# One stage of a fused two-block kernel: an output turned by TensorE is instead moved between partitions by small DMAs

## The reference

```
u  = h @ w_in                                   # 256 x 1024
bu = einsum('sbgk,gpk->sbgp', u by groups, b)   # complex: 64 groups, 64 states each, 16 inputs each
x_t = a * x_{t-1} + bu_t                        # complex diagonal recurrence over the 256 positions
y  = Re(einsum('sbgp,gkp->bsgk', x, c)) + d_skip * u
y  = gelu(y)
y  = y * sigmoid(y @ w_glu)
out = y @ w_o
```

## Time and profile before

| | before |
|---|---|
| median of three runs | 2977.66 us (2976.47 to 2978.38) |
| the profiled execution's own time | 2976.47 us |
| its span | 2974.7 us |
| TensorE busy | 2838.1 us (95%) |
| VectorE busy | 1879.9 us (63%) |
| ScalarE busy | 1341.9 us (45%) |
| mean granted TensorE clock | 0.971 of full speed |

### The profile page before, as it was taken

How to read it: one execution, slowest core, us unless ns; L and a number is a source line. 1 busy time by engine, 2 the same in 40 slices (tenths; PEclk the granted TensorE clock), 3 DMA queues, 4 the chain that set the end, 5 groups by cost and what they waited for, 6 DMA issues and landing times.

```text
span 2974.7 us, 42854 instructions
## 1 busy us (share of the span) xinstructions
PE 2838.1 (95%) x17486; PEld 2547.6 (86%) x17487; DVE 1879.9 (63%) x2146; ACT 1341.9 (45%) x1380; POOL 275.3 (9%) x248
## 2 busy tenths in 40 slices
PE   6988999898999999999998999999999999998999
PEld 4857988887888888888877998888899999996999
DVE  5474454546898888887453653785566466485655
ACT  1222431215777777776443432343544444345444
POOL 0002862300000000000001000002100010010000
PEclk8968999898999999999999999999999999999999
DMA  7845674355999999998462563433456456472553
GB/s 238 272 158 151 187 222 134 96 197 192 336 376 336 341 341 377 335 340 315 170 211 87 180 202 118 141 114 113 133 183 201 139 170 208 150 186 80 181 180 110
DMA packets 504835, 609.84 MB, mean 205 GB/s; under 512 B 50201, under 2 KB 371836, under 8 KB 504700
## 3 DMA queue, kind: packets, MB, share of 16 engines
q1 hardware_dynamic: 502224, 606.82, 61.1%
q10 hardware_dynamic: 2476, 1.06, 0.1%
HBM read 605.75 MB, written 1.05 MB: 204 GB/s over the span
## 4 chain that ended last, share of the span: by engine, by line
PE 85%; DVE 5%; DMA 3%; issue 2%; ACT 2%; POOL 1%; SPq 0%; DVEq 0%; ACTq 0%; POOLq 0%
PE bank L1423 31%; PE bank L1986 7%; PE bank L1832 4%; PE bank L1836 4%; PE bank L1845 4%; PE bank L1250 4%; PE bank L1745 3%; PE bank L1302 3%; PE bank L1894 2%; PE bank L1885 2%; PE bank L1886 2%; DMA ring<-in_o_exp_down 1%; PE bank L1750 1%; PE bank L1920 1%; DVE ring L3085 1%
## 5 line engine op out<-in xcount | busy, mean ns | idle before, releaser
L3189 DVE TENSOR_TENSOR ring_r<-ring,store_area_r 128x2048 fp32r<-128x2048 f32 (+1 forms) x344 | 805.5, 2379 | 228.0 <-ACT store_area_r L2397 225.1
L2397 ACT ACTIVATE store_area_r<-ring 128x2048 fp32r<-128x2048 f32 (+1 forms) x344 | 665.5, 1971 | 235.9 <-PE bank L1423 81.3
L1423 PE MATMUL bank<-sq_r,store_area_r 128*128 128x256 f32 x1648 | 241.6, 288 | 13.0 <-ACT sq_r L2401 8.0
L1423 PE MATMUL bank<-sq_r,ring_r 128*128 128x256 f32 x1664 | 236.4, 285 | 0.0
L1423 PE MATMUL bank<-hT_r,store_area_r 128*128 128x256 f32 x1648 | 233.3, 285 | 0.0
L1423 PEld LDWEIGHTS bank<-sq_r,store_area_r 128*128 128x128 f32 x1648 | 217.1, 193 | 18.5 <-issue 9.0
L1986 PE MATMUL bank<-hT,ring 128*128 128x256 f32 x1024 | 230.0, 380 | 0.0
L3631 DVE TENSOR_TENSOR ring_r<-ring,store_area_r 128x3072 fp32r<-128x3072 f32 x64 | 195.0, 3088 | 47.2 <-ACT store_area_r L2795 47.2
L1423 PEld LDWEIGHTS bank<-sq_r,ring_r 128*128 128x128 f32 x1664 | 217.4, 194 | 0.0
L1423 PEld LDWEIGHTS bank<-hT_r,store_area_r 128*128 128x128 f32 x1648 | 214.8, 194 | 0.0
L1986 PEld LDWEIGHTS bank<-hT,ring 128*128 128x128 f32 x1024 | 190.8, 190 | 27.1 <-issue 3.1
(11 more groups left out here) (545 smaller groups left out, 4762.6 us busy)
## 6 DMA issues: line engine op xcount, KB each, us to landing
ring<-in_o_exp_gate SPq DMA_DIRECT2D x88, 1024.0 KB, 7.1
ring<-in_o_exp_up SPq DMA_DIRECT2D x88, 1024.0 KB, 7.2
ring<-in_ffn_w_gu SPq DMA_DIRECT2D x88, 1024.0 KB, 6.7
ring<-in_o_exp_down SPq DMA_DIRECT2D x32, 1536.0 KB, 8.5
ring<-in_ffn_w_down SPq DMA_DIRECT2D x32, 1408.0 KB, 8.7
ring<-in_o_exp_down SPq DMA_DIRECT2D x32, 1280.0 KB, 11.3
ring<-in_ssd_w_in SPq DMA_DIRECT2D x32, 1024.0 KB, 7.1
ring<-in_e_mod_mix_w SPq DMA_DIRECT2D x12, 1024.0 KB, 9.1
```

Source lines behind the costliest of these rows:

```text
L1423: i = mm(out, w(k), x(k), start=(p == k == 0), stop=(p == 2 and k == blocks - 1))
L2397: activation(dst, slot(u, s, kk), ACT.Copy).then_inc(w_high, 1)
L3189: nc.vector.tensor_tensor(slot(u, s, kk, rounded=True), slot(u, s, kk), as_f(high), ALU.subtract).then_inc(w_low, 1)
```

## The change

The output y gets the orientation in which the inputs came: rows (j, 32 features) and columns (b, t). The tables become the stationary side with 128 columns, and the state and `u` the moving side with 63 and 64. ACT copies PSUM (128 x 256) in one piece to one of four `y_raw` buffers, and then 16 DMAs for each tile (`outputs_moved`), of 32 partitions x 256 bytes each, bring it to rows (b, 32 features): 8 issued by SP, 8 by ACT. The transposes on PE are gone. The semaphore `moved` becomes two. The skip sum of tile j comes one round later on DVE, and waits for the DMAs. The state is stored unshifted, in contiguous tiles. On PE the two later halves of the `u` product move into the loop, one in m = 0 and one in m = 1; on ACT the evacuation of tiles 4 to 7 and its DMAs follow the copy and the DMAs of tile 0. On SP the loads for glu 1 and two mod units are placed between the DMAs.

```
+    def outputs_moved(eng, issue, m, phases):
+        eng.wait_ge(moved[m % 2], MOVES * (m // 2 + 1))
+        for j in phases:
+            for b in range(4):
+                issue.dma_start(y_nat(m)[32 * b:32 * b + 32, j * S5_B:(j + 1) * S5_B],
+                                y_raw(m)[32 * j:32 * j + 32, b * S5_B:(b + 1) * S5_B]).then_inc(moved[m % 2], 16)
...
-    y_raw = lambda m, h: ring[0:S5_B, 2 * (m % 2) + h, (KD + 2) * COLS:(KD + 3) * COLS]
+    y_raw = lambda m: ring[:, m % 4, (KD + 2) * COLS:(KD + 3) * COLS]
...
                 if stage == "s5_glu":
                     glu_units(0, 1)
-                    sp.wait_ge(evac, base["s5_in"] + 2)
-                    inputs_moved(sp, nc.sync, 1, (0, 1))
-                    glu_units(1, 4)
+                    for m in range(S5_M):
+                        if m == 1:
+                            sp.wait_ge(evac, base["s5_in"] + 2)
+                            inputs_moved(sp, nc.sync, 1, (0, 1))
+                            glu_units(1, 3)
+                        sp.wait_ge(y_cp, m + 1)
+                        outputs_moved(sp, nc.sync, m, (0, 1))
+                    glu_units(3, 4)
...
-                    pe.wait_ge(moved, MOVES * (m // 4 + 1))
+                    pe.wait_ge(moved[m // 4], MOVES)
...
-                    y = y_banks[m % 2][0:S5_B, :].rearrange("p (j b c) -> p j b c", j=S5_L, b=4)
+                    y = y_banks[m % 2]
                     for b in range(4):
-                        at = slice(b * S5_B, (b + 1) * S5_B)
-                        mm(y[:, :, b, :], u_rel(m)[:, at], s5_direct(m)[:, b, :].rearrange("p (j c) -> p j c", c=32), start=True, stop=False)
+                        i, at = 4 * m + b, b * S5_B
+                        mm(y[:, at:at + S5_B], s5_direct(m)[:, b, :], u_rel(m)[:, at:at + S5_B], start=True, stop=False)
                         for n in range(2):
-                            ins = mm(y[:, :, b, :], s5_p[m % 2][:, n, at], s5_ct[n][:, 4 * m + b, :, :], start=False, stop=(n == 1))
+                            ins = mm(y[:, at + 1:at + S5_B], s5_ct[n][:, i, :, :].rearrange("p j c -> p (j c)"),
+                                     s5_p[m % 2][:, n, at:at + S5_B - 1], start=False, stop=(n == 1))
...
-                for s in range(2):
-                    later_half(s)
-                pe.wait_ge(bc_cp, before + S5_M)
                 for m in range(S5_M):
+                    if m < 2:
+                        later_half(m)
                     if m + 2 < S5_M:
                         inputs(m + 2)
                     outputs(m)
-                    if m >= 1:
-                        outputs_turned(m - 1)
-                outputs_turned(S5_M - 1)
...
-                unit_in(1)
                 for m in range(S5_M):
+                    if m == 1:
+                        unit_in(1)
                     se.wait_ge(w_used, m + 1)
-                    if m >= 2:
-                        se.wait_ge(y_turned, m - 1)
-                    for half in range(2):
-                        ins = activation(y_raw(m, half), y_banks[m % 2][0:S5_B, half * T:(half + 1) * T], ACT.Copy)
-                    ins.then_inc(y_cp, 1)
+                    if m >= 4:
+                        se.wait_ge(y_read, m - 3)
+                    activation(y_raw(m), y_banks[m % 2][:, 0:T], ACT.Copy).then_inc(y_cp, 1)
+                    se.wait_ge(y_cp, m + 1)
+                    outputs_moved(se, nc.scalar, m, (2, 3))
                     if m >= 2:
                         gelu(m - 2)
...
-                    if m >= 4:
-                        j = m - 4
-                        ve.wait_ge(y_turned, j + 1)
-                        nc.vector.scalar_tensor_tensor(out=y_nat(j), in0=u_nat(j), scalar=vcol("o_d_skip", j), in1=y_turn(j),
+                    if m >= 5:
+                        j = m - 5
+                        ve.wait_ge(moved[j % 2], MOVES * (j // 2 + 2))
+                        nc.vector.scalar_tensor_tensor(out=y_nat(j), in0=u_nat(j), scalar=vcol("o_d_skip", j), in1=y_nat(j),
```

More of the change, by code:

```diff
@@ L149, in program @@
     (s5_act, s5_dve, s5_tr, s5_cols, range_ready, ple_half, tab_ready, raw_in, c_raw_in, b0_ready, bw_ready, c_exp, c_powers,
-     bc_tr, bc_cp, y_cp, y_turned) = (sem(n) for n in (
+     bc_tr, bc_cp, y_cp) = (sem(n) for n in (
         "s5_act", "s5_dve", "s5_tr", "s5_cols", "range_ready", "ple_half", "tab_ready", "raw_in", "c_raw_in", "b0_ready",
-        "bw_ready", "c_exp", "c_powers", "bc_tr", "bc_cp", "y_cp", "y_turned"))
-    moved = sem("moved")
+        "bw_ready", "c_exp", "c_powers", "bc_tr", "bc_cp", "y_cp"))
+    moved = [sem(f"moved{i}") for i in range(2)]
     bu_ready, bu_turned, turned, scanned, back_c, w_ready, w_used, y_read, y_gelu, glu_sig = (
@@ L320, in inputs_moved @@
                 issue.dma_start(to[:, :, b * S5_B:(b + 1) * S5_B],
-                                act[32 * b:32 * b + 32, 4 * i:4 * i + 4, j * S5_B:(j + 1) * S5_B]).then_inc(moved, 16)
+                                act[32 * b:32 * b + 32, 4 * i:4 * i + 4, j * S5_B:(j + 1) * S5_B]).then_inc(moved[i], 16)
+    def outputs_moved(eng, issue, m, phases):
[4 more added lines that the diff above has]
+                                y_raw(m)[32 * j:32 * j + 32, b * S5_B:(b + 1) * S5_B]).then_inc(moved[m % 2], 16)
     EPS_COL, FB_COL, DTB_COL, ALOG_COL = 0, 1, 2, 3
@@ L442, in program @@
     v_banks, d_banks, y_banks = (bank_x, bank_sum), banks[d_set:d_set + 2], banks[y_set:y_set + 2]
-    y_turn = lambda m: (d_banks if m < S5_M - 2 else v_banks)[m % 2][:, 0:T]
     BT_CHUNKS, C_CHUNKS = 2 * S5_M, 4
@@ L1661, in outputs @@
                     pe.wait_ge(back_c, m + 1)
-                    y = y_banks[m % 2][0:S5_B, :].rearrange("p (j b c) -> p j b c", j=S5_L, b=4)
+                    y = y_banks[m % 2]
                     for b in range(4):
-                        at = slice(b * S5_B, (b + 1) * S5_B)
-                        mm(y[:, :, b, :], u_rel(m)[:, at], s5_direct(m)[:, b, :].rearrange("p (j c) -> p j c", c=32), start=True, stop=False)
+                        i, at = 4 * m + b, b * S5_B
+                        mm(y[:, at:at + S5_B], s5_direct(m)[:, b, :], u_rel(m)[:, at:at + S5_B], start=True, stop=False)
                         for n in range(2):
-                            ins = mm(y[:, :, b, :], s5_p[m % 2][:, n, at], s5_ct[n][:, 4 * m + b, :, :], start=False, stop=(n == 1))
+                            ins = mm(y[:, at + 1:at + S5_B], s5_ct[n][:, i, :, :].rearrange("p j c -> p (j c)"),
+                                     s5_p[m % 2][:, n, at:at + S5_B - 1], start=False, stop=(n == 1))
                     ins.then_inc(w_used, 1)
-                def outputs_turned(m):
-                    pe.wait_ge(y_cp, m + 1)
-                    if m >= 2:
[L1673 to L1677, removed]
                 def later_half(s):
@@ L3511, in s5_in @@
                 ve.wait_ge(tab_ready, NS // 8)
[L3512 to L3516, removed]
+                for m in range(S5_M + 5):
                     if 2 <= m <= S5_M + 1:
@@ L3520, in s5_in @@
                         tally.wait(ve)
-                        p, q = later(s5_p[j % 2]), earlier(s5_q[j % 2])
-                        nc.vector.tensor_tensor(p[:, 0], p[:, 0], q[:, 1], ALU.subtract)
-                        nc.vector.tensor_tensor(p[:, 1], p[:, 1], q[:, 0], ALU.add).then_inc(back_c, 1)
+                        p, q = s5_p[j % 2], s5_q[j % 2]
+                        nc.vector.tensor_tensor(p[:, 0, :], p[:, 0, :], q[:, 1, :], ALU.subtract)
+                        nc.vector.tensor_tensor(p[:, 1, :], p[:, 1, :], q[:, 0, :], ALU.add).then_inc(back_c, 1)
                     if m < S5_M:
@@ L3544, in s5_in @@
                             ve.wait_ge(w_used, j - 1)
-                        cosines = s5_cos[:, 4 * j:4 * j + 4, 0:S5_B - 1].rearrange("p (c b) t -> p c b t", c=1)
-                        tally.up(nc.vector.tensor_tensor(later(s5_p[j % 2]), earlier(s5_w[j % 2]),
-                                                         cosines.to_broadcast([P, 2, 4, S5_B - 1]), ALU.mult))
-                    if m >= 4:
-                        j = m - 4
-                        ve.wait_ge(y_turned, j + 1)
-                        nc.vector.scalar_tensor_tensor(out=y_nat(j), in0=u_nat(j), scalar=vcol("o_d_skip", j), in1=y_turn(j),
+                        cosines = flat2(s5_cos[:, 4 * j:4 * j + 4, :]).rearrange("p (c t) -> p c t", c=1).to_broadcast([P, 2, T])
+                        tally.up(nc.vector.tensor_tensor(s5_p[j % 2], s5_w[j % 2], cosines, ALU.mult))
+                    if m >= 5:
+                        j = m - 5
+                        ve.wait_ge(moved[j % 2], MOVES * (j // 2 + 2))
+                        nc.vector.scalar_tensor_tensor(out=y_nat(j), in0=u_nat(j), scalar=vcol("o_d_skip", j), in1=y_nat(j),
                                                        op0=ALU.mult, op1=ALU.add).then_inc(y_read, 1)
```

1 line of the change is left out of this document (removed).

## The result

Before: 2978.02 us (median of 6 runs, 2976.36 to 2982.12). After: 3000.62 us (6 runs, 2995.23 to 3009.21). The ratio is 1.0078, 95% interval 1.0064 to 1.009: **slower by 22.6 us**, against +9.9 forecast and outside the range of 2979 to 2992. The profiled execution of after took 3007.69 us, its span is 3005.9 us and the mean granted clock 0.959 (before: 0.971).

A forecast was written before the change was run, and what follows sets the result against it. TensorE was busy 95% of the span, with DVE's 6.23 us round pacing the stage; later glu 0 through ACT's issues (+8.2) and the low clock (+1.7) gave +9.9, forecast 2987 us, range 2979 to 2992.

The forecast's parts named there:

- TensorE and the order: In the S5 loop: tiles follow at DVE's 6.23 us a round; glu 0 could start 2.3 us earlier if nothing else were late.
- The last rival: SP and ACT issues delay each other: some 30 us, or milder with slow landing and low clock, 2990; chance 0.14.
- nothing gained: PE's 24 `outputs` instructions with 128 weight and 64 moving columns take 2.6 to 2.8 us, as the last `outputs` does now.
- Tile 4's arrival: Ahead of `inputs(4)`: ACT's eighth DMA issued at 564.7, landed 2.0 later at 566.7, `inputs(4)` done at 568.7.
- longer landing: Tile 4's DMAs land after 3.3 instead of 1.9 us, costing 1.4 us; part of a milder case with 2990.
- ScalarE: On ACT: 8 issues at 0.68 make a round 6.6 us, over DVE's 6.23; glu 0 ends 8.2 us later.
- signs in PE: Glu 0's first product starts near 601, PE idles twice inside it for ACT's gelu, and the granted clock dips behind that.
- cheap-issue rival: On ACT: 0.47 us a DMA, a round of 4.9 us; +2.7, with the clock up to +4.4, 2979 to 2982; chance 0.22.
- another price: On ACT: by the Trainium skill's DMA setup cost, eight issues would take some 2 to 3 us.
- SP and ACT hold each other up: As one shared unit, an issue costs up to 1.25 us, an ACT round 11.1, the end some 30 us; chance 0.14.
- The interleaving pays: At 0.3 us or less an issue, ACT keeps up and tile 4 comes 1.7 earlier: -4 us, 2973.5; chance 0.06.
- term of 1.7 for the clock: In glu 0, after PE stands nearly idle for 11 us: 64 instructions at low clock take 15.56 instead of 13.82, +1.7 us.

The follow-up runs named there:

- b_act_issues: The kernel before with 8 idle DMAs of 32 partitions x 256 bytes behind each of ACT's copies, from ACT's own list: 2992.11 us, ratio 1.0033.
- a_wide_old_order: The changed kernel with products of 128 moving columns, and the later halves, their evacuation and DMAs back in front of the loop: 2993.66 us, ratio 1.0042.
- a_wide: The changed kernel with `inputs` and `outputs` products of the first three blocks widened to 128 moving columns, same results and count: 2993.47 us, ratio 1.0043.
- after_again: The changed kernel measured once more, unchanged: 3000.50 us, ratio 1.0066.
- a_old_order: The changed kernel with the later halves, their evacuation and DMAs back in front of the loop, output DMAs kept: 3004.63 us, ratio 1.0077.
- a_no_act_dmas: The changed kernel without ACT's 8 output DMAs of each tile, so half of y's columns are not moved: 2998.01 us, ratio 1.0062.
- a_late_loads: The changed kernel with SP's 4 MB of weight loads issued at m = 4 instead of m = 1: 3000.63 us, ratio 1.0065.
- a_filled: The changed kernel with 8 unused 512-column products in PE's wait for tile 4 and one behind the outputs of tiles 2 to 6: 3002.56 us, ratio 1.0084.
- b_filled: The kernel before with 3 unused 512-column products in PE's wait ahead of `inputs(0)`: 2977.79 us, ratio 0.9992.

## Why the prediction was wrong

**The sum, in its own terms.** Forecast part: 77.15 + 9.9 = 87.05. Measured: 99.7. With the stage starts laid on each other (3.8 us off all positions of after):

| step | forecast | measured | miss |
|---|---|---|---|
| DVE takes tile 4 | 568.7 | 574.0 | +5.3 |
| DVE takes tile 7 | 587.4 | 599.6 | +6.9 more |
| from there to copy(7) on ACT | 19.5 | 19.0 | -0.5 |
| from copy(7) to the end of glu 0 | 20.1 | 21.1 | +1.0 |

The misses add up to 12.7, the whole difference.

- **TensorE and the order: the step that failed.** It read "from there at 6.23 a round, tile 5 comes at 574.9, 6 at 581.2, 7 at 587.4". That is DVE's round, and it holds only while PE keeps under it. At the low clock PE needs 5.1 us for an `outputs` and 3.4 for an `inputs`, 8.53 together. The last rival had an `outputs` at the low clock in one round or so (5.6, with `inputs` at 2.0); it was in all three, and `inputs` was slow as well. What the forecast did not ask is what the new form of the products would do to the clock. It costed that form as "nothing gained" by instruction time alone, which at full clock is right. Its own rows had a sign: the two rounds from 568.99 to 582.28 take 13.29 us and not 12.46, and DVE's idle 0.75 us there is put down to PE. PE was already over DVE's round every other time, in the rounds at clock 0.76.
- **Tile 4's arrival.** The 8 issues on ACT took 6.60 us and not 5.46, so the last began at 565.5 and not at 564.7 (+0.8); it landed 4.7 us later and not 2.0 (+2.7), and `inputs(4)` took 3.7 us and not 2.0 (+1.7). That is the +5.3, to 0.1. The text's longer landing was 3.3; 4.7 is beyond it.
- **ScalarE: right.** The issues take 0.59 to 0.61 us in the median and 0.66 to 0.69 apart, against 0.68 assumed. ACT's last rounds are 6.2 to 6.4 us against 6.6, and the term measured by itself is +9.5 against +8.2 to +9.9. The signs in PE came out otherwise: glu 0 began at 616.5 (620.3 less the 3.8) and not near 601, because of the slow rounds, and PE idled once inside it (4.33 us, for gelu 5) and not twice. The cheap-issue rival is dead: no issue of L328 under 0.507 us, 8 of them 5.0 us or more, neither 3.8 nor the 2 to 3 that the prediction names as another price. So is the thought that SP and ACT hold each other up: the medians of 64 issues on each are 0.591 and 0.613.
- **The interleaving pays: wrong in sign.** The new order alone costs before +4.8 in the part and +0.17% (interval 0.07 to 0.26). In after no cost is shown: with wide products the parts differ by 3.3 and the ratios by 0.0001, with narrow ones the parts are 96.6 against 96.5 to 99.7.
- **Behind the wait.** glu 0's last 54 instructions took 14.6 us where 11.8 was forecast at full clock; the term of 1.7 for the clock became 2.7.

**Where the 22.6 us come from**, step by step from before to after, by the part and by the ratio:

| kernel | what is added | part | ratio |
|---|---|---|---|
| before | | 77.1 | 1 |
| b_act_issues | issues on ACT | 86.7 (+9.5) | 1.0033 |
| a_wide_old_order | the new outputs with their moves, without the transposes | 90.1 (+3.4) | 1.0042 |
| a_wide | the new order | 93.4 (+3.3) | 1.0043 |
| after, after_again | narrow products | 96.5 to 99.7 (+3.1 to +6.3) | 1.0066 to 1.0078 |

The second step changes several things at once, and no steps but the first and last stand clear of noise: the issues on ACT, about 10 us, and the narrow products, 7 to 10 us by the ratios. Against full clock the rounds and `inputs(4)` lose 8.6 us in the part. That removing the narrow products gives back less there is probably because ACT's list is then the bound; this is argued, not shown.

**The cause of the low clock.** Shown: it needs neither the order nor the wait (a_old_order), nor ACT's DMAs (a_no_act_dmas), nor the weight loads (a_late_loads), it is not prevented by filling the wait (a_filled), and with the same number of products at 128 columns the rounds return from 8.53 to about 6.4 us in both orders. Not shown: what in the narrow products lets it fall in mid-loop. The clock is granted by the chip and the profile only reports it. The Trainium skill ("TensorE: Matmul & The Clock Gate", Part 1: The HAM clock gate) describes a clock that is throttled until the engine is active enough. By the busy time in this profile that would speak against after's rounds: PE is busy 8.50 of 8.50 us at 0.50. The row decides, and it says that a PE that the profile calls busy can stay at the low level: here from 574 to 624, with one gap of 1.55 us.

**Open.** Why the landing of tile 4's inputs varies between executions; why the medians of the kernels without ACT's DMAs gain less than their parts; what the new outputs and the new order cost by themselves in after; why one product of 512 columns a round did not hold the clock. Fewer and larger DMAs for a tile were not tried.

## What to carry to other kernels

A DMA costs the engine that issues it, here 0.6 us each: eight of them in ScalarE's own list made it the bound of a stretch in which it had been busy 15.3 of 77 us, so count issues as work of that engine. When the form of a product changes, ask of the granted clock as well as of the instruction's time: on a loop whose bound is another engine, TensorE's slack hides a price at full clock and not at half. A wait filled with unused products, or products widened where columns are free, is a cheap thing to try wherever the clock row dips. Here, in the kernel before, both together were worth 0.12%.

## What the runs showed of the hardware

- Products of 128 weight columns by 63 or 64 moving columns, from 574.1 to 620.3 with one gap of 1.55 us, were all run at the granted clock 0.50 (after); with 128 moving columns the clock came back, to a mean of 0.87 over four rounds (a_wide).
- Products take the same time with 64 and with 128 moving columns at either clock: 2.00 and 1.95 us for 16 instructions of `inputs` at full clock, 0.64 us for two of `outputs` at 0.50. The added columns were free.
- Three products of 512 columns in a wait of 2.8 us kept the clock at 1.00 behind it: the next 32 instructions, unchanged, took 3.73 instead of 6.56 us (b_filled).
- A small DMA between partitions takes its issuer at least 0.51 us and 0.59 to 0.61 in the median, with single ones up to 1.3 on ACT and 2.7 on SP, for one run of 256 bytes a partition (L328 of after). With 4 runs it took 0.60 and 0.63 before the change, 0.61 and 0.66 after it.
